# Two halves of four heads in each level of a triangular inversion, in place of one group of eight

## The reference, cut to what matters

```python
def rwkv7_scan(r, w, k, v, a, b):
    def step(st, inp):
        r_t, w_t, k_t, v_t, a_t, b_t = inp
        sa = jnp.einsum('bhvk,bhk->bhv', st, a_t)
        st = st * w_t[:, :, None, :] + sa[..., None] * b_t[:, :, None, :] + v_t[..., None] * k_t[:, :, None, :]
        y = jnp.einsum('bhvk,bhk->bhv', st, r_t)
        return st, y
    ...
    _, ys = lax.scan(step, s0, xs)
```

## Time and profile before

| | |
|---|---|
| median of 3 runs | 4204.16 us |
| lowest, highest | 4185.85, 4207.37 us |
| profiled execution, its own time | 4187.31 us |
| its span, first to last instruction | 4186.0 us |
| mean granted TensorE clock in the span | 0.945 |
| instructions | 75909 |

### The profile page before, as it was taken

The page is one execution under the profiler, slowest core; times in us unless marked ns, Lnnn a source line. Parts: engine busy times, 40 slices in busy tenths (PEclk is TensorE's granted clock), DMA queues, the critical chain, the costliest instruction groups (busy, mean ns, idle before and its releaser), DMA issues. The chain is left out here.

```text
span 4186.0 us, 75909 instructions
## 1 busy us (share of the span) xinstructions
PE 3873.8 (93%) x33370; PEld 3177.9 (76%) x33370; DVE 2265.3 (54%) x3675; ACT 1196.0 (29%) x1698; POOL 449.7 (11%) x440
## 2 busy tenths in 40 slices
PE   6999969888999999999999999787788999999998
PEld 5888847777867888888798677566676788888887
DVE  4643345555434666766625333465654476666675
ACT  5221234333223433121401322243323321111123
POOL 0001103231000442000000000231311000000000
PEclk9999979999999999999999999788878999999999
DMA  5211120113122334322323412201004211111112
GB/s 183 84 60 49 61 99 6 33 30 138 41 77 74 103 117 162 128 95 83 111 96 122 143 63 86 77 28 54 23 30 140 104 51 41 51 41 61 41 61 81
DMA packets 230589, 327.11 MB, mean 78 GB/s; under 512 B 17372, under 2 KB 171740, under 8 KB 230132
## 3 DMA queue, kind: packets, MB, share of 16 engines
q1 hardware_dynamic: 201616, 259.52, 18.7%
q10 hardware_dynamic: 28644, 62.72, 3.9%
HBM read 239.66 MB, written 82.54 MB: 77 GB/s over the span
## 5 line engine op out<-in xcount | busy, mean ns | idle before, releaser
L471 PE MATMUL ps<-sb_a_h,sb_whi 128*128 128x512 f32 (+1 forms) x2336 | 931.5, 399 | 5.1 <-DVE sb_wlo L432 5.1
L473 PE MATMUL ps<-sb_a_h,sb_whi 128*128 128x512 f32 (+1 forms) x2336 | 915.0, 392 | 0.0
L472 PE MATMUL ps<-sb_a_h,sb_wlo 128*128 128x512 f32 (+1 forms) x2336 | 914.5, 391 | 0.0
L471 PEld LDWEIGHTS ps<-sb_a_h,sb_whi 128*128 128x128 f32 (+1 forms) x2336 | 441.3, 189 | 113.2 <-issue 15.8
L472 PEld LDWEIGHTS ps<-sb_a_h,sb_wlo 128*128 128x128 f32 (+1 forms) x2336 | 441.4, 189 | 95.2 <-issue 4.9
L473 PEld LDWEIGHTS ps<-sb_a_h,sb_whi 128*128 128x128 f32 (+1 forms) x2336 | 440.7, 189 | 94.8
L422 ACT ACTIVATE sb_whi<-sb_wraw 128x2048 fp32r<-128x2048 f32 (+2 forms) x129 | 233.1, 1807 | 764.7 <-PE ps L473 494.0
L677 DVE TENSOR_TENSOR sb_x<-sb_x,ps 128x512 f32<-128x512 f32 x480 | 314.9, 684 | 211.3 <-PE ps L473 196.6
L432 DVE TENSOR_TENSOR sb_wlo<-sb_wraw,sb_whi 128x2048 fp32r<-128x2048 f32 (+2 forms) x129 | 281.7, 2184 | 220.5 <-ACT sb_whi L422 200.9
L471 PE MATMUL ps<-sb_a_g,sb_whi 128*128 128x512 f32 x864 | 337.4, 390 | 11.5 <-DVE sb_x L677 10.5
L472 PE MATMUL ps<-sb_a_g,sb_wlo 128*128 128x512 f32 x864 | 336.2, 389 | 0.0
(11 more groups left out here) (599 smaller groups left out, 6728.3 us busy)
## 6 DMA issues: line engine op xcount, KB each, us to landing
sb_wraw<-w_in SPq DMA_DIRECT2D x33, 1024.0 KB, 5.3
sb_wraw<-w_ff SPq DMA_DIRECT2D x32, 1024.0 KB, 5.5
sb_wraw<-w_up SPq DMA_DIRECT2D x22, 1024.0 KB, 5.1
sb_wraw<-w_down SPq DMA_DIRECT2D x11, 1024.0 KB, 4.9
sb_wraw<-w_xkv SPq DMA_DIRECT2D x8, 1024.0 KB, 5.4
sb_wraw<-w_out SPq DMA_DIRECT2D x8, 1024.0 KB, 5.3
sb_b<-rw_d SPq DMA_DIRECT2D x16, 512.0 KB, 6.4
sb_b<-y SPq DMA_DIRECT2D x16, 512.0 KB, 5.7
```

Source lines behind the costliest of these rows:

```text
L471: e.matmul(o, wh[:, k, c], xh[:, sl], start=(k == 0), stop=False)
L472: e.matmul(o, wl[:, k, c], xh[:, sl], start=False, stop=False)
L473: m = e.matmul(o, wh[:, k, c], xl[:, sl], start=False, stop=(k == t.nk - 1))
```

## The change

Each level is done in two halves, g = 0 (heads 0 to 3) and g = 1 (heads 4 to 7). Half 0 of Y and X takes bank 0, half 1 takes bank 1, each with that bank's own counts. The second part of X goes beside the first in half 0's bank, and for half 1 into a bank of its own out of the ring (2, 3) under the key `rw_xa`. The loops have g outermost now, then q, then c. VectorE evicts each half with instructions of half the size. As other keys still take both banks under bank 0's count, `pair_room` makes them wait for the last half in bank 1, and `half_room` makes half 1 wait for the last pair. Other uses of the pair (`rw_mb`, `rw_qb`, `rw_t`, `rw_w`, `rw_a`) call `pair_room` and are otherwise as before.

```diff
+            last_pair, second_half = [None], [None]
+
+            def pair_room(e, key):
+                bk.take(key, PAIR)
+                last_pair[0] = key
+                if second_half[0]:
+                    e.wait_ge(*bk.emptied(second_half[0]))
+                e.wait_ge(*bk.room(key))
+                return bk.pair(key)
+
+            def half_room(e, key, g):
+                ps = bk.take(key, (g,))
+                if g:
+                    e.wait_ge(*bk.emptied(last_pair[0]))
+                    second_half[0] = key
+                e.wait_ge(*bk.room(key))
+                return ps
+
...
                 for lv, b in enumerate(LEVELS):
-                    e.wait_ge(*bk.emptied(("rw_x", i, lv - 1) if lv else ("rw_t", i)))
                     if lv == 0:
+                        e.wait_ge(*bk.emptied(("rw_t", i)))
                         e.wait_ge(*rw_xa0.at(i))
-                    bk.take(("rw_y", i, lv), PAIR)
-                    ps = bk.pair(("rw_y", i, lv))
-                    e.wait_ge(*bk.room(("rw_y", i, lv)))
-                    for c, g, q in quarters():
-                        m = e.matmul(quarter(ps, 1 - c if g else c, g, q, 64), block(R(M, 512), c, 4 * g + q),
-                                     block(R(XT, 512), c, 4 * g + q), start=True, stop=True)
-                    m.then_inc(*bk.fill(("rw_y", i, lv)))
-                    yield
-                    e.wait_ge(*bk.emptied(("rw_y", i, lv)))
-                    bk.take(("rw_x", i, lv), PAIR)
-                    ps = bk.pair(("rw_x", i, lv))
-                    e.wait_ge(*bk.room(("rw_x", i, lv)))
-                    for c, g, q in quarters():
-                        o = 1 - c if g else c
-                        m = e.matmul(v3(quarter(ps, c, g, q, 32), b), block(R(XA, 512), o, 4 * g + q),
-                                     second(block(R(Y, 512), o, 4 * g + q), b, 1), start=True, stop=True)
-                    if lv < 4:
-                        for c, h in blocks():
-                            m = e.matmul(v3(small(ps[:, 0, 128:384], c, h), b), block(R(Y, 512), c, h),
-                                         second(block(R(XA, 512), c, h), b, 0), start=True, stop=True)
-                    m.then_inc(*bk.fill(("rw_x", i, lv)))
-                    yield
-                e.wait_ge(*bk.emptied(("rw_x", i, 4)))
+                    for g in range(2):
+                        key = ("rw_y", i, lv, g)
+                        ps = half_room(e, key, g)
+                        if lv:
+                            e.wait_ge(*bk.emptied(("rw_xa", i, lv - 1) if g else ("rw_x", i, lv - 1, g)))
+                        for q in range(4):
+                            for c in range(2):
+                                o = 1 - c if g else c
+                                m = e.matmul(ps[64 * o:64 * o + 64, 64 * q:64 * q + 64], block(R(M, 512), c, 4 * g + q),
+                                             block(R(XT, 512), c, 4 * g + q), start=True, stop=True)
+                        m.then_inc(*bk.fill(key))
+                    yield
+                    for g in range(2):
+                        key = ("rw_x", i, lv, g)
+                        ps = half_room(e, key, g)
+                        e.wait_ge(*bk.emptied(("rw_y", i, lv, g)))
+                        for q in range(4):
+                            for c in range(2):
+                                o = 1 - c if g else c
+                                m = e.matmul(v3(small(ps[:, 0:128], c, q), b), block(R(XA, 512), o, 4 * g + q),
+                                             second(block(R(Y, 512), o, 4 * g + q), b, 1), start=True, stop=True)
+                        if lv < 4:
+                            if g:
+                                m.then_inc(*bk.fill(key))
+                                key = ("rw_xa", i, lv)
+                                ps = bk.take(key, ONE_BANK)
+                                e.wait_ge(*bk.room(key))
+                            for q in range(4):
+                                for c in range(2):
+                                    m = e.matmul(v3(small(ps[:, 128:256], c, q), b), block(R(Y, 512), c, 4 * g + q),
+                                                 second(block(R(XA, 512), c, 4 * g + q), b, 0), start=True, stop=True)
+                        m.then_inc(*bk.fill(key))
+                    yield
+                for g in range(2):
+                    e.wait_ge(*bk.emptied(("rw_x", i, 4, g)))
...
                 for lv, b in enumerate(LEVELS):
-                    e.wait_ge(*bk.filled(("rw_y", i, lv)))
-                    e.tensor_tensor(gq(R(Y, 512)), split(bk.pair(("rw_y", i, lv)), 0), m24(f"LT{b}"), ALU.mult).then_inc(*bk.empty(("rw_y", i, lv)))
-                    yield
-                    pair = bk.pair(("rw_x", i, lv))
-                    x = R(XT, 512).rearrange("p (g n z b) -> p g n z b", g=2, z=2, b=b)[:, :, :, 1]
-                    e.wait_ge(*bk.filled(("rw_x", i, lv)))
-                    e.tensor_tensor(x, x, pair[:, :, 0:128].rearrange("p g (n b) -> p g n b", b=b),
-                                    ALU.subtract).then_inc(*(vo.up() if lv < 4 else bk.empty(("rw_x", i, lv))))
-                    if lv < 4:
-                        x = second(R(XA, 512), b, 0)
-                        e.tensor_tensor(x, x, v3(pair[:, 0, 128:384], b), ALU.subtract).then_inc(*bk.empty(("rw_x", i, lv)))
+                    for g in range(2):
+                        key = ("rw_y", i, lv, g)
+                        e.wait_ge(*bk.filled(key))
+                        e.tensor_tensor(v6(R(Y + 256 * g, 256)), v6(bk[key][:, 0:256]), b3(C(f"LT{b}"), 4, 64),
+                                        ALU.mult).then_inc(*bk.empty(key))
+                    yield
+                    for g in range(2):
+                        key = ("rw_x", i, lv, g)
+                        x = second(R(XT + 256 * g, 256), b, 1)
+                        e.wait_ge(*bk.filled(key))
+                        e.tensor_tensor(x, x, v3(bk[key][:, 0:128], b),
+                                        ALU.subtract).then_inc(*(bk.empty(key) if g or lv == 4 else vo.up()))
+                        if lv < 4:
+                            if g:
+                                key = ("rw_xa", i, lv)
+                                e.wait_ge(*bk.filled(key))
+                            x = second(R(XA + 256 * g, 256), b, 0)
+                            e.tensor_tensor(x, x, v3(bk[key][:, 128:256], b), ALU.subtract).then_inc(*bk.empty(key))
                     yield
```

More of the change, by code:

```diff
@@ L3609, in pe_blocks @@
                 m.then_inc(*bk.fill(key))
+            last_pair, second_half = [None], [None]
[13 more added lines that the diff above has]
+                return ps
             def pe_features(e, key, products):
-                bk.take(key, PAIR)
-                ps = bk.pair(key)
-                e.wait_ge(*bk.room(key))
+                ps = pair_room(e, key)
                 for at, a, b in products:
@@ L3804, in pe_in @@
                 yield
-                bk.take(("rw_t", i), PAIR)
-                ps = bk.pair(("rw_t", i))
                 e.wait_ge(*rw_x0.at(i))
-                e.wait_ge(*bk.room(("rw_t", i)))
+                ps = pair_room(e, ("rw_t", i))
                 for c, h in blocks():
```

## The result

The changed kernel takes 4166.67 us (median of 11 runs), the kernel before, over as many runs, 4192.71. One of the changed kernel's runs, 5556.12 us at a clock of 0.64, is left out of everything that follows (the median of the other ten is 4165.8). The ratio is 0.9934 with a 95% interval of 0.9921 to 0.9947: faster by 0.66%, some 28 us. The forecast was 4210 us and no change that can be measured; the range ended at 4168, and "faster" had a chance of 0.20. The profiled execution took 4164.4 us, span 4162.7 (before 4187.31 and 4186.0).

The account below looks back on a forecast made before the run. TensorE was taken to bound the kernel, busy 93% of the span. The terms 46 - 16 - 16 + 3 + 2 = +19 and the clock's -13 gave +6 us on the median 4204.16: 4210 us, range 4168 to 4248.

Parts of the forecast that it names:

- the sum without the clock: All terms of the mixer's stage except the clock's: 46 - 16 - 16 + 3 + 2 = +19 us.
- Order inside a group: Y and X's first part use two array quarters in turn, not four, at L3849's pace: +46 us of TensorE time.
- Waits removed: Before Y and X, half 1 on TensorE covers half 0's eviction: -16 us, bounds 0 and -28.
- VectorE's +3: Smaller evictions add 17 us to VectorE, mostly beside TensorE's work; where VectorE is late they count: +3 us.
- Absorbed: Longer groups are free where TensorE waits for something else, 8 us in long waits and 8 at L3992: -16 us.
- Clock: In the mixer's stage, filled gaps raise TensorE's mean granted clock by 0.04: -13 us, bounds 0 and +0.13 of clock.
- The base: Whole kernel before the change: median of three runs, 4204.16 us, on which the forecast difference was put.
- The clock rival: Filled gaps keep the clock up in first and last units, stage mean 0.93: -23 us, 4181; chance 0.17.
- TensorE's time in full: Stage clock stays at 0.80 and half of what is called absorbed is on the path: +33 us, 4237; chance 0.27.
- the ring: Bank (2 or 3) of X's second part is late at level 3, in eight units: about +30 us, 4234; chance 0.05.
- fills gaps with longer groups: Basis of the clock gain: stage's TensorE busy time goes from 389 of 480 us to about 435 of 499.
- VectorE, +17 us busy: Evictions in halves in the mixer's stage: Y +6 us, X +11 us, with 128x128 priced at 0.286 us.

Follow-up runs that it names:

- e1: The kernel before with only the matmul order inside Y and X's first part changed, g outermost, one eviction and one wait as before; 0.9983 of the kernel before.
- e6: The kernel before with Y and X's first part ordered one quarter of the array at a time (g, then c, then q); 1.0134 of the kernel before.
- e8: The changed kernel with one unneeded matmul more in each of 32 levels, ahead of X's second part of half 1; 0.9977 of the kernel before.
- e9: The kernel before, levels untouched, with unneeded matmuls into a free bank ahead of TensorE's waits of rw_mb, rw_t, first rw_a and output's turn; 0.9982 of the kernel before.
- e2: The changed kernel, but the first half of Y and of X waits until both halves of what it reads are evicted; 0.9970 of the kernel before.

## Why the prediction was wrong

The direction of the clock, its price and its rival were right. The order and the clock were mis-sized, a third term, what would be absorbed, was not there at all, and of the two large errors both point the same way. Term by term, beside the means at one clock: the sum without the clock was +19 and measured +2, the clock was -13 and measured -30. So +6 became -28.

- **Order inside a group, "40 x 0.606 + 40 x 0.544 = +46.0 us".** This step failed; it measured 11. I took L3849's pace for the new groups, as if a group ended before the next began. e1's timeline shows 0.28 us more for Y and 0.07 for X's round at full clock, some 14 us in all, and e1 costs 11 us at one clock. The rise in busy time by the two lines (71.3 to 100.4) is no measure of it, since lines that run at once are counted each. I had seen 1.02 against 0.56 and did not ask whether the other two quarters stayed empty at the seams. The rule of the Trainium skill (TensorE: Matmul & The Clock Gate, part 3, "The mechanism") that I weighed with it speaks of weight loads that overlap matmuls of other row groups; that the new order would then cost nothing was my own step from it. The runs bear out the overlap (32 loads take 0.84 us alternating in e1, 1.40 in e6) and not that step: two quarters in turn do cost something against four.
- **Waits removed, -16.** With VectorE's +3, 13 net; measured from e1 to the changed kernel at one clock: 11.0 - 1.7 = 9 us, of which 5 by smaller evictions and 4 by own-half waits. Idle before the levels fell by 9.5 us in the profile, not 16: the long waits before Y are left, as said, and of the plain ones before X more than I had taken.
- **Absorbed, -16.** This term failed too: 14 us or more of added issue came out as 11, and the wait that was to take 8 of it, that of the output's turn, is as long as before (9.6 and 10.0 us). It stood against the order's error and hid a part of it.
- **Clock, "+0.04: -13 us".** Right in sign and unit price: 3.2 us for one hundredth of the stage's clock. By the runs it is 2.9 us for 0.001 of the span's, and the inversion is some 450 of 4180 us, so 3.1 for a hundredth. The size failed: it was 0.07 in the two profiles, over 480 us, and if the whole rise of the span's clock in the mean of the runs lay in the inversion, 0.0104 x 4180 / 450 = 0.097; I took 0.04 and bounded it at 0.13. I had fitted the slope over stretches of 60 us, which average the ends with the middle; the two stretches in which nearly only the levels stood went from 0.50 to 0.93 and 1.00, and I had named them for the rival alone.
- **The base, 4204.16 us.** Over 11 runs the kernel before takes 4192.71. Three runs had given a median 11 us too high, and I put the change on it. With the better base the forecast would have been 4199, so a quarter of the distance between 4210 and 4166.67 is the base and three quarters the terms above; the result lies 1.3 us below the range's end, and the base alone is more than that.
- **The rivals.** The clock rival, 23 us faster by the clock, is the nearest to what happened, and in part by luck: the pair of profiles shows the stage at 0.87, short of the 0.93 from which it was to decide, and the order, which it priced at 46 as I did, made up the rest. The sum of "TensorE's time in full" does not follow its own words: half of the absorbed term and the waits unchanged give 46 - 16 - 8 + 3 + 2 = +27, not +33. "TensorE's time in full" and the ring are refuted (e1; no wait of L3874 for L3711). The clock's basis, "fills gaps with longer groups", is not shown: e8 and e9 have more work and a higher clock, but e6 has the longest groups and a lower one. What sets the clock in the levels stays open.
- **VectorE, +17 us busy:** 128x128 took 280 ns where I had bounded it by 286; 292.89 against 274.69 us. Right.

In the profile pair alone, TensorE at the stage's clock 0.87, the idle fall and the ends' clock could be read at once; that it was the clock and not the waits could not. That took e1, e2, e9 and the comparison at one clock.

## What to carry to other kernels

Where TensorE is near the edge between its two clock levels, note the granted clock of every run beside its time, and compare kernels at one clock; an edit's own cost and its effect on the clock may be of opposite sign and of equal size. A stretch in which a short chain of small matmuls and evictions stands alone is where such a clock is lost and won: look at it by itself, not in an average. And the pace of a group inside a stream is read from the start of the first to the end of the last of the whole round, as groups in different parts of the array overlap.

## What the runs showed of the hardware

- Matmuls of 64x64 in other quarters of the array start before earlier ones of the program: L3864's records amid L3874's at 3103.49 us. One quarter at a time costs less than its count of turns for the same reason: in e6 a Y took 1.40 us at full clock, where 1.85 had been worked out. Its loads start 58 ns apart, but 1 to 4 ns where one quarter's work meets the next one's.
- The granted clock is not a matter of TensorE's busy time by its records: 417.99 us of 480 at 0.78 (e6), 405.77 at 0.85 (e9), 389.00 at 0.80 (before), 387.93 at 0.87 (after), and 402.46 at 0.92 in e8's run of the highest clock. The Trainium skill (TensorE: Matmul & The Clock Gate, part 1, "What's actually happening") has the gate follow how busy the array has been; these rows don't follow the busy time that the records show, and how the two are related isn't settled here.
- 2.9 us for each 0.001 of the span's clock (2.5 to 3.4 in the kernels with 10 runs or more) is most of the spread between runs of one kernel: before, 4175.56 us at 0.949 to 4215.97 at 0.937.
